# Block 0 of the first half goes ahead: the output projection between the last attention heads, queries for its 128 tokens alone, expert choice and row fetches earlier, and eight standing places for rows instead of five

## The reference, cut to what matters

```python
hn = rmsnorm(x, mix_norm_w)                       # x: 512 tokens x 1024
z, xbc, dt_raw, q, k, v = split(hn @ w_in)
y_ssd  = ssd_branch(z, xbc, dt_raw, ...)          # conv (width 4) + silu, chunked scan
y_diff = diff_attention(q, k, v, ...)             # 4 heads x 2 maps, blocks of 128 queries
x = x + concat([y_ssd, y_diff]) @ w_out           # output projection
xb = rmsnorm(x, ffn_norm_w)
q  = xb @ w_q                                     # 8 heads x 2 halves x 128
sc = q . sub_keys                                 # 128 keys per half
# per token and head: top 16 of each half, top 16 of the 16x16 sums -> 16 of 16384 experts
h  = gelu(xb . u[idx]);  x = x + sum(softmax(s) * h * v[idx])
```

## Time and profile before

| | us |
|---|---|
| three runs | 1398.34, 1396.46, 1395.39 (median 1396.46) |
| the profiled execution's span | 1396.6 |
| busy in it: PE, DVE, POOL, ACT | 1364.6 (98%), 1083.6 (78%), 610.1 (44%), 435.3 (31%) |
| DMA moved | 467.69 MB, 335 GB/s on the mean |

### The profile page before, as it was taken

One profiled execution on the slowest core, in us unless ns is written; L12 is line 12 of the kernel. 1 busy time (PEld: TensorE's weight loads), 2 busy tenths in 40 slices (PEclk: granted clock), 3 DMA queues, 4 the chain that ended last, 5 costly groups with the idle time before them and its releaser, 6 DMA issues.

```text
span 1396.6 us, 16311 instructions
## 1 busy us (share of the span) xinstructions
PE 1364.6 (98%) x5402; PEld 933.1 (67%) x5402; DVE 1083.6 (78%) x2469; ACT 435.3 (31%) x1219; POOL 610.1 (44%) x516
## 2 busy tenths in 40 slices
PE   7999999999998999999999999999999999999998
PEld 5656648566587888888899999995444444444443
DVE  4535445899899999999999999998777677766656
ACT  2533532544411111112787887872000000000000
POOL 0000001733855444434466655664577645754440
PEclk9999999999999999999999999999999999999999
DMA  8322234975999999989899999999999999999997
GB/s 321 140 107 99 116 149 172 371 287 208 406 366 407 375 332 384 326 302 316 296 394 400 403 405 385 391 384 389 363 409 409 409 409 409 410 409 409 410 409 308
DMA packets 121763, 467.69 MB, mean 335 GB/s; under 512 B 13776, under 2 KB 14160, under 8 KB 115152
## 3 DMA queue, kind: packets, MB, share of 16 engines
q0 software_dynamic: 73728, 268.47, 49.9%
q1 hardware_dynamic: 47664, 197.66, 36.6%
q10 hardware_dynamic: 288, 0.52, 0.1%
HBM read 462.67 MB, written 3.93 MB: 334 GB/s over the span
## 4 chain that ended last, share of the span: by engine, by line
PE 60%; DMA 22%; DVE 9%; issue 3%; POOL 3%; ACT 2%; another core or an unknown queue 0%; DVEq 0%; SPq 0%; ACTq 0%; POOLq 0%
PE BANKS L929 32%; PE BANKS L729 11%; PE BANKS L721 9%; DMA BIG<-v,IDX 7%; DMA BIG<-u,IDX 7%; DMA UV<-v,IDX 4%; PE BANKS L948 4%; DMA UV<-u,IDX 2%; POOL BIG L1665 2%; DVE X L1623 1%; POOL UV L1665 1%; DVE BIG L1618 1%; DVE UV L1618 1%; DMA T<-away 1%; PE BANKS L912 1%
## 5 line engine op out<-in xcount | busy, mean ns | idle before, releaser
L1665 POOL DMA_INDIRECT UV<-u,IDX x153 | 184.1, 1203 | 411.1 <-DVE IDX L1495 263.3
L1665 POOL DMA_INDIRECT UV<-v,IDX x159 | 191.1, 1202 | 121.0 <-DVE X L1623 51.2
L1623 DVE SCALAR_TENSOR_TENSOR X<-UV,HG,X 128x1024 f32<-128x1024 f32 x159 | 203.9, 1282 | 40.7 <-DMA UV<-v,IDX 36.3
L929 PE MATMUL BANKS<-T 128*128 128x256 f32 x1024 | 229.2, 379 | 1.0 <-issue 1.0
L953 PE MATMUL BANKS<-T,BIG 128*128 128x512 f32 x512 | 225.2, 592 | 0.2 <-DMA T<-v 0.2
L953 PE MATMUL BANKS<-Y,BIG 128*128 128x512 f32 x512 | 225.1, 592 | 0.0
L929 PE MATMUL BANKS<-T,Y 128*128 128x256 f32 x992 | 221.9, 379 | 0.0
L1618 DVE SCALAR_TENSOR_TENSOR UV<-UV,Y 128x1024 f32<-128x1024 f32 x153 | 186.3, 1221 | 42.5 <-DMA UV<-u,IDX 37.7
L929 PEld LDWEIGHTS BANKS<-T 128*128 128x128 f32 x1024 | 192.0, 190 | 26.1 <-issue 1.4
L929 PEld LDWEIGHTS BANKS<-T,Y 128*128 128x128 f32 x992 | 186.0, 190 | 24.0
L953 PEld LDWEIGHTS BANKS<-Y,BIG 128*128 128x128 f32 x512 | 97.3, 190 | 122.5 <-issue 122.5
(11 more groups left out here) (272 smaller groups left out, 1243.6 us busy)
## 6 DMA issues: line engine op xcount, KB each, us to landing
T<-u_t SPq DMA_DIRECT2D x64, 512.0 KB
T<-v SPq DMA_DIRECT2D x64, 512.0 KB
Y<-v SPq DMA_DIRECT2D x64, 512.0 KB
Y<-u_t SPq DMA_DIRECT2D x62, 512.0 KB
BIG<-w_in SPq DMA_DIRECT2D x23, 1024.0 KB, 4.8
BIG<-w_q SPq DMA_DIRECT2D x16, 1024.0 KB, 6.9
BIG<-w_out SPq DMA_DIRECT2D x8, 1024.0 KB, 4.9
UV<-v,IDX POOLq DMA_INDIRECT x159
```

What stands on the lines that cost most here:

```text
L929: last = nc.tensor.matmul(PS[(i + 2) % 4][:, 0:HT], ub[:, c, :], T8[:, 1, c, :], start=(c == 0), stop=(c == KC - 1))
L1623: stt(xb, row, HG[:, n % 2, i % UNIT:i % UNIT + 1], xb, ALU.mult, ALU.add).then_inc(used, 1)
L1665: pool.indirect_dma_start(row_place(s), None, u if kind == "ru" else v, bass.IndirectOffsetOnAxis(IDX[:, b, c:c + 1], 0)).then_inc(row_in[ ...
```

## The change

In `ORDER`: `x15` stands right behind `x14`. `R0` of block 0 stands between heads 5 and 6 of the attention (behind `cv8`), `cv9` between heads 6 and 7. For blocks 0 and 1 the order behind head 7 is now `R1` of block 0, `T1`, `R0` of block 1, `U0`, `R1` of block 1, then the new step `Wa` (pieces 0 to 3 of the queries for block 0's 128 tokens alone), `U1`, `K0`; the first choice (`r0`, `r1`, `y0`, `yc0`) follows, and `W0` to `W3` now compute only the other 128 tokens. `k2` and `k3` move behind them, and the weight tile list follows. The second choice (`r2`, `r3`, `y1`, `yc1`), which stood among heads 9 to 12, now stands among the scan and projections of blocks 2 and 3 and ahead of head 8. The rows are spread anew. `RING` is 8 instead of 5 (12 KB more per partition), and the kernel asks for 4096 bytes of descriptor scratch for indirect DMAs where the default stood. `rows()` now stops ahead of a `ru` whose unit has no indices yet. No product, norm or choice is left out or added; four query pieces are computed in two halves of 128 columns.

```diff
-RING = 5
+RING = 8
...
+            if item[0] == "ru" and item[1] >= known[0] * UNIT:
+                break
...
-            then = after.get(i, [])
-            ahead = ended or i == 6
-            out += then[:1] + on("C", i) if ahead else on("C", i)
+            out += before.get(i, []) + on("C", i)
             if (i + 1) % DH == 0:
                 out += on("nq", i // DH)
-            out += then[1:] if ahead else then
+            out += after.get(i, [])
...
-    after[7] += on("N n2", 1) + on("R0", 0) + on("T", 1) + many("cv", 8, 10) + on("R1 Q", 0) + many("cv", 10, 12)
-    after[7] += on("R0", 1) + many("cv", 12, 14) + on("F", 0) + on("R1 Q", 1) + on("U", 0) + on("F", 1) + on("k", 2)
-    after[7] += on("U", 1) + on("k", 3)
+    before = {4: many("x", 13, 14), 6: many("cv", 8, 9) + on("R0", 0)}
...
+    after[5] = many("x", 14, 16)
+    after[6] = many("cv", 9, 10)
+    after[7] = on("N n2", 1) + on("R1 Q", 0) + on("T", 1) + many("cv", 10, 12) + on("F", 0) + on("R0", 1) + on("U", 0)
+    after[7] += many("cv", 12, 14) + on("R1 Q", 1) + on("F", 1) + many("Wa", 0, 4) + on("U", 1) + many("K", 0, 1)
...
+    o += many("cv", 14, 16) + pick(0) + many("W", 0, 4) + on("k", 2) + many("K", 1, 2) + on("k", 3) + on("ks k1", 1) + rows(4)
...
+    o += on("q", 2) + on("S2", 2) + on("q", 3) + on("S3", 2) + on("D", 3) + rows(3) + on("S1", 3) + [first] + on("M", 3) + on("qs q1", 1) + rows(1)
+    o += on("v", 2) + on("q2", 1) + on("v", 3) + [second] + on("S2", 3) + many("qt", 6, 8) + on("S3", 3) + rows(1) + [keys]
+    at_start = many("W", 8, 9) + [columns]
...
+        def query_tokens(step, i):
+            return slice(0, P) if step == "Wa" else slice(P if i < 4 else 0, HT)
...
-                    last = nc.tensor.matmul(bank[:, 0:HT], wt, src[:, c, :], start=(c == 0), stop=(c == KC - 1))
+                    last = nc.tensor.matmul(bank[:, tok], wt, src[:, c, :], start=(c == 0), stop=(c == KC - 1))
...
-    nc = bacc.Bacc("TRN2", target_bir_lowering=False, num_devices=1)
+    nc = bacc.Bacc("TRN2", target_bir_lowering=False, num_devices=1, dynamic_dma_scratch_size=4096)
```

More of the change, by code:

```diff
@@ L101, in work_order @@
     place = [0]
+    known = [LATE]
     def rows(m):
@@ L118, in work_order, with attention @@
     o += on("k2", 0) + on("v", 1) + many("qt", 0, 4)
-    def attention(first, end, after, between):
+    def attention(first, end, before, after, between):
         out = on("A", first) + on("A", first + 1) + between[:1] + on("c", first) + between[1:]
@@ L162, in second_attention @@
         return out
-    after = {i: many("x", 9 + i, min(10 + i, 16)) for i in range(8)}
-    after[4] += on("T", 0)
-    after[7] += on("N n2", 1) + on("R0", 0) + on("T", 1) + many("cv", 8, 10) + on("R1 Q", 0) + many("cv", 10, 12)
-    after[7] += on("R0", 1) + many("cv", 12, 14) + on("F", 0) + on("R1 Q", 1) + on("U", 0) + on("F", 1) + on("k", 2)
-    after[7] += on("U", 1) + on("k", 3)
-    o += attention(0, 8, after, on("x", 8))
+    before = {4: many("x", 13, 14), 6: many("cv", 8, 9) + on("R0", 0)}
+    after = {i: many("x", 9 + i, 10 + i) for i in range(4)}
+    after[4] = on("T", 0)
+    after[5] = many("x", 14, 16)
+    after[6] = many("cv", 9, 10)
+    after[7] = on("N n2", 1) + on("R1 Q", 0) + on("T", 1) + many("cv", 10, 12) + on("F", 0) + on("R0", 1) + on("U", 0)
+    after[7] += many("cv", 12, 14) + on("R1 Q", 1) + on("F", 1) + many("Wa", 0, 4) + on("U", 1) + many("K", 0, 1)
+    o += attention(0, 8, before, after, on("x", 8))
     def pick(n):
@@ L173, in pick @@
         return many("r", b * PH + 2 * q, b * PH + 2 * q + 2) + on("y yc", n)
[L175 to L179, removed]
+    o += many("cv", 14, 16) + pick(0) + many("W", 0, 4) + on("k", 2) + many("K", 1, 2) + on("k", 3) + on("ks k1", 1) + rows(4)
+    o += many("W", 4, 8) + many("K", 2, 4) + rows(9)
+    o += on("z", 2) + on("D", 2) + on("k2", 1) + on("S1", 2) + on("z", 3) + many("qt", 4, 6) + rows(4) + on("M", 2) + rows(6)
     first, second, keys, columns = pick(1)
-    between = {9: [first], 10: [second], 11: [keys], 12: [columns] + rows(1)}
+    o += on("q", 2) + on("S2", 2) + on("q", 3) + on("S3", 2) + on("D", 3) + rows(3) + on("S1", 3) + [first] + on("M", 3) + on("qs q1", 1) + rows(1)
+    o += on("v", 2) + on("q2", 1) + on("v", 3) + [second] + on("S2", 3) + many("qt", 6, 8) + on("S3", 3) + rows(1) + [keys]
+    at_start = many("W", 8, 9) + [columns]
     after = {}
     for i in range(8, 16):
-        after[i] = many("W", i + 1, min(i + 2, 16)) + (between[i] if i in between else rows({8: 3, 13: 1, 14: 3, 15: 0}[i]))
+        after[i] = many("W", i + 1, min(i + 2, 16)) + rows({12: 4, 13: 1, 15: 0}.get(i, 3))
     after[15] = on("T", 2)
@@ L709, in x_weights, with channels @@
                 return W[:, (n + cb % 4 // 2) % NHALFW, at:at + P]
-            def channels(half, cb, n, bank, signal, halves=(), weights=None):
-                src = T8[:, half]
+            def channels(half, cb, n, bank, signal, halves=(), weights=None, tok=slice(0, HT)):
+                src = T8[:, half, :, tok]
                 for c in range(KC):
@@ L895, in _ @@
                            turned(i))
-                elif step == "W":
-                    half, j = i // (2 * PH), i % (2 * PH)
-                    if j % 4 == 0:
+                elif step in ("Wa", "W"):
+                    half, j, first = i // (2 * PH), i % (2 * PH), 1 if step == "Wa" else 4 * (i // (2 * PH)) + 3
+                    if j % 4 == 0 and (step, i) != ("W", 0):
                         n = weights_in()
-                    channels(half, j, n, PS[w_bank(i)] if w_bank(i) > 1 else bank_01(w_bank(i), q2_done, i + 1), q2_full,
-                             [(ut_done, 4 * half + 3 + c) for c in range(2)])
+                    at = QUERIES[(step, i)]
+                    channels(half, j, n, PS[w_bank(i)] if w_bank(i) > 1 else bank_01(w_bank(i), q2_done, at + 1), q2_full,
+                             [(ut_done, first + c) for c in range(2)], tok=query_tokens(step, i))
                 elif step == "K":
```

25 lines of the change are left out of this document (15 added, 10 removed).

## The result

The changed kernel took 1414.2 us (median of four runs, 1408.7 to 1420.1) against 1397.3 us of the kernel before (median of four): ratio 1.0118, 95% interval 1.0089 to 1.0148. It is slower, as forecast, but by 16.9 us where the sum gave 10.7: 2.2 us above the forecast's own range (1401 to 1412) and 1.2 us above the wider one (to 1413). The profiled execution has a span of 1411.2 us and a time of 1413.05; an execution's time is thus about 1.8 us more than its span, and the span of 1396.6 of the kernel before belongs to its run of 1398.34, so that it does not stand for that run's time. The runs of the changed kernel lie 11 us apart, those of the kernel before 3.

The account below looks back on a forecast made before the run. The prediction took PE, without waits in the dense part, as the bound, with rows ending within half a microsecond of it. 1396.6 + 6.4 + 8.1 - 2.0 - 1.8 = 1407.3 us, range 1401 to 1412.

Parts of the forecast that it names:

- so it costs nothing: First choice ahead of k1: it moves into DVE's idle 24.89 us, at no cost, and rows start nearly 20 us sooner.
- rival 4: Pauses at W8 and B8: the clock falls after them, one query piece loses 3.5 us, 1410.8 us in all; chance 0.06.
- Per tile nothing changes on PE: Dense part: PE's work per tile stays the same, while thirteen more rows are done at the last gl tile.
- First half, +6.4: PE up to z2: new waits at C7, R0, R1 and W0 and half-width queries add 6.4 us.
- the half-width pieces: Block 0 and 1 queries: eight half pieces cost 0.8 us more by the row, 0 if halves cost half; 0.4 taken.
- Second choice, +8.1: Ahead of head 8: DVE has 8.1 us more between S1 of block 3 and the maxima; PE waits at W8 and B8.
- DVE, full there, has no way to catch up: Behind B8: DVE's orders carry the same load as before, so the 8.1 us lost ahead of it stay lost.
- The end, -2.0: Kernel's end: rows end earlier than PE, only the last of four additions follows PE, giving 2.0 us back.
- the stall, -1.8: PE's unexplained 3.59 us wait behind ACT, ahead of the dense part: between 0 and -3.6 us, taken as -1.8.
- rival 1: Rows are the true bound of the end and front waits shrink: faster, 1389.7 us; chance 0.10.
- can take away only what lies behind PE's end: Dense part and end: finishing rows earlier gains only behind PE's end, since PE has no wait there to give back.
- Rival 5: Smaller descriptor scratch or 16 crowded places slow POOL, so rows end last: 1416 us; chance 0.05.

Follow-up runs that it names:

- e11: Kernel before with eight places, 4096 bytes of scratch and eight more row steps ahead of the third one-hot: 1404.2 us, ratio 1.0034 to the kernel before.
- e3: Changed kernel with one DVE step moved, the copy D2 ahead of nine rows instead of behind them: 1414.0 us, ratio 1.0093 to the kernel before.
- e5: Changed kernel with 19 row steps moved from between the gl tiles to behind the third one-hot: 1413.0 us, ratio 1.0100 to the kernel before.
- e6: Changed kernel with D2 ahead of the nine rows and 19 rows moved behind the third one-hot: 1405.2 us, ratio 1.0053 to the kernel before.
- e7: Changed kernel without the thirteen early rows ahead of z2 and with six fewer between gl tiles: 1402.1 us, ratio 1.0024 to the kernel before.
- e10: Changed kernel with second-half rows and second choice as before, and cv9 behind head 7: 1398.9 us, ratio 0.9997 to the kernel before.
- e8: Kernel before with 4096 bytes of descriptor scratch and its five standing places: 1400.2 us, ratio 1.0014 to the kernel before.
- e1: Kernel before with eight standing row places and 4096 bytes of descriptor scratch, order untouched: 1391.2 us, ratio 0.9941 to the kernel before.

## Why the prediction came out right in sign and wrong in size

- **Base.** The sum was made on the span, 1396.6, and compared with run times; the median of the kernel before is 1397.3. 0.7 us of the miss of 6.9 is this slip; 6.2 lie in the terms.
- **PE's way to the first `gl` tile: the step that failed.** The forecast had 12.7 us here (6.4 + 8.1 - 1.8); measured from head 0's scores the profiled execution has 19.9 (347.2 against 327.3). Its terms, from the rows above: first half 5.7, wait for `D2` 4.1, waits at `W8` and `B8` 5.2, lower clock 8.0, the stall gone -3.6; together 19.4. The wait for `D2` and the clock had been put at nothing, and they are 12.1 us.
- **The wait for `D2`.** Of the moved rows I costed only the idle time that they fill ("so it costs nothing"). The thirteen that now stand ahead of `D2` wait for DMA, and with them PE, 4.07 us and 2.6 more at the lower clock (1.84 in the scan's matmuls, 0.78 in `z3`); moving `D2` gave 6.0 us back at the first `gl` tile.
- **The clock.** I gave rival 4 a chance of 0.06 on the strength of one pause of 3.59 us with no fall behind it ("by the rows alone it loses nothing"). In the changed kernel the clock falls at four places ahead of the first `gl` tile, for 1.7 to 2.6 us each; rival 4 had the mechanism, with one fall of 3.5. The Trainium skill (TensorE: Matmul & The Clock Gate, Part 1) says that an idle array is put back to 1.2 GHz. The falls behind these pauses agree with that, and the pause of the earlier trace rows, which no fall followed, does not.
- **The dense part: a second step that failed.** "Per tile nothing changes on PE" and PE "has no wait left in the dense part" were true of the trace, but I did not ask how far behind PE the next engine stood. It was 1.7 us at the third `og`. I counted thirteen more rows at the last `gl` tile and used them only for the end, where they looked like a gain; the 19 ahead of the third one-hot are 23 us of DVE work. `e11` shows that DVE takes up none of such rows, and `e3`, `e5` and `e6` that this bound and PE's way hide each other: 3.5 and 2.5 us by the ratios for either alone, within their intervals of nothing, 9.1 for both. In the changed kernel the two end within 0.16 us of each other, so either step alone would have given its time. `e6` stays 4.1 us above `e7`; its early rows are still there, and its wait at `W8` is 4.88 us instead of 3.50.
- **First half, +6.4.** Right in sum, and nearly so by terms: `C7` 2.75 us (+2.3, forecast +2.6), `R0` of block 1 0.66 (0.8), `U0` 0.87 (0.2 more than the wait before), `R1` of block 1 0.74 (0.9), `W0` 0.69 (with its neighbours some 1.4, forecast 1.7); the half-width pieces cost 1.0 (7.64 + 7.41 us against 14.05) where I took 0.4 and the row said 0.8. Sum at `z2` 5.7 without a fall of the clock, 7.4 with one at `C7`; in time 7.3. `e10` shows that the wait is not `cv9`'s alone: DVE's and ACT's load there moves it to `U0`.
- **Second choice, +8.1.** The mechanism was right (`B8` and `W8` wait for DVE), the term too large: 7.0 at `B8`, 1.7 of it clock, 5.3 at the first `gl` tile, 4.3 in time. The step "DVE, full there, has no way to catch up" failed by 1.7 us in `e7`, and part of the rest lies under the wait at the third `og`.
- **The end, -2.0, and the stall, -1.8.** Both went the forecast way and were too small: -3.6 each in the profiled execution (6.8 to 3.2 behind PE's end, and 3.59 gone). In the kernel before the rows are one bound of the end, as rival 1 said, and five places are what binds them: `e8` loses the stall and gains nothing, `e1` gains 8.3 us with the places. The sentence that earlier rows "can take away only what lies behind PE's end" left out the one-hots, through which late rows hold PE in `e8`. Rival 5, which had the places as a loss, had the wrong sign. What stalled ACT stays open; no other profiled execution here has it.

Added up by the ratios, with the forecast behind each: places -8.3 (end and stall, -3.8), first half +7.3 (+6.4), second choice +4.3 (+8.1), early rows and the 19 rows ahead of the one-hots +13.1 (nothing), together +16.4 (+10.7). The terms that the forecast had come to +3.3 alone (`e7`, 1.0024); most of the measured loss is the term that it did not have. That the forecast came within some 6 us of the loss is luck.

## What to carry to other kernels

When work is moved ahead of a point, add it up for every engine that has to arrive there, and read the slack of the second-latest, not only the wait of the latest: an engine that shows no wait can stand 1.7 us from being the bound. Where an edit that removes a plain wait changes nothing, look downstream for a wait that has grown by the same amount before the theory is given up, and undo two suspects together. Give every new pause of PE a second price, the clock behind it, from rows of the same work at both levels. And of a change with many parts, try first the one that touches no order: here the standing places alone were worth 0.6%, and the rest of the change cost three times that.
